# The Fourier part of a hybrid encoder layer: its last product turned round, with features in partitions and 257 frequencies

## The chip, the cores and the metric

The kernel runs on one core of a Trainium2 chip. The metric is the device time of one execution in microseconds (us); the time of a kernel is the median of its runs. PE is the TensorE matmul pipe and PEld its weight load, DVE is VectorE, ACT is ScalarE, POOL is GpSimd, and SP is SyncE, whose queue ("SPq") issues nearly all DMAs.

## The reference

One encoder layer on 512 tokens of 1024 features in float32: x gains W_out times the concatenation of three mixers of the normed x (gated linear attention, GLA, 256 features; Fourier, 256; latent attention, MLA, 512), and then a mixture of 32 experts is added. The Fourier mixer is this:

```python
def fnet_mixer(u, w_mix):            # u: 512 tokens x 256 features = 4 groups of 64
    uf = u.astype(jnp.float32).reshape(B, S, FNET_GROUPS, FNET_DG)
    f = jnp.fft.fft2(uf, axes=(1, 3), norm='ortho').real
    y = jnp.einsum('bsgc,gcd->bsgd', f, w_mix.astype(jnp.float32))
    return y.reshape(B, S, FNET_W).astype(u.dtype)

x = x + jnp.concatenate([o_gla, o_fnet, o_mla], axis=-1) @ w_out[l]
x = x + hier_moe(rms_norm(x, norm2_g[l]), ...)
```

The real part is C u Cc - S u Ss, where C and S are the cosine and sine transforms over the tokens and Cc and Ss those over the 64 channels of a group. Over the tokens C u is even and S u is odd about frequency 256.

## The kernel before, in words

Each engine runs a program of its own, written out in order (the `block.sync`, `block.tensor`, `block.scalar`, `block.vector` and `block.gpsimd` functions); semaphores join them. The eight PSUM banks are given out by a plan, `psum_plan` (line 69): `use(key, bank)` notes for every product its bank and how often the bank must have been filled and freed by then. `open_bank` waits until the product before in that bank was read, `filled` waits for a product, `free_bank` counts a read, and `drained(eng, key)` makes an engine wait until a product was read.

The order is: the input projection; GLA; the Fourier part and MLA; the output projection with W_out, tile by tile of 128 tokens, with the routing; the 32 experts in pairs, with the weights of 7 experts held at a time; the sum and the last norm.

The Fourier part. The tokens are folded in two halves (sum and difference), and four products `AB` (line 949) give cosine and sine transforms of two blocks of 128 features at 129 even or 128 odd frequencies. `spectrum` (line 565) is used by ScalarE (lines 1424 to 1428) and VectorE (`copy_spectrum`, line 1779) to copy each product twice into the tile `AB` (cosine or sine, block, 512 frequencies): once as it is and once mirrored for the upper frequencies. The matrices `fM` are the channel transforms multiplied by the mixing weights, with a third, negated copy of the sine one for the upper half. Behind the first set of scores TensorE forms `fy` (line 994): for each tile of 128 frequencies, with the frequencies in partitions, 2 blocks x 2 products of 128x128. ScalarE copies each tile to `MIX[:, t, 256:512]` (`copy_fy`, line 1430). GLA's output stands in `MIX[:, t, 0:256]`; GpSimd multiplies it by its gate there (line 2148) and raises `gla_out`.

MLA. `attention_order` (line 184) writes out TensorE's order: for each of 8 sets `s`, four score tiles of 128x512 (`scores`, line 974: a part without rope, one with, one without; lines 958 and 969), into banks 0 to 3. In sets 3 and 4 two transposes `mT` of MIX each follow (line 1030: 4 transposes per bank), which put the four blocks of 128 mixed features into partitions, for W_out. Then come the product with V for set s-2 (`AV`, line 1047) and the transposes of the probabilities of set s-1 (`PT`, line 1036). The `pre` steps, behind the last set, begin the output projection (line 1002). The other engines follow the same order by hand: VectorE takes each row's maximum (`row_max`, line 1804) and scales the probabilities (`normalise`, line 1808: a reciprocal at line 1810, a scaling at line 1811); ScalarE takes the exponentials (`exponent`, line 1434), which free banks 0 to 3, and copies the transposed probabilities (`copy_probs`, line 1442). The four `mT` products are copied to `xnT` by ScalarE (line 1461) and VectorE (line 1821).

SyncE waits at line 638 for the last `fy` tile to have been copied and for `gla_out`, and then issues the loads of the final gain, of W_out (lines 641, 642; over the tile AB), and of the weights of experts 2 and 3. It waits for the four `mT` (line 655) before it loads expert 4's gate and up weights over MIX, and then for the attention's outputs before the next loads.

Of the kernel before, what the change touches and what calls it, by code (L numbers as in the profile page):

```python
# [30 lines left out]
ALU = mybir.AluOpType  # L31
# [3 lines left out]
P = 128  # L35
# [21 lines left out]
PAIRS = NE // 2  # L57
SETS, MIX_TURNS = 8, (3, 4)

# [9 lines left out]
def psum_plan():  # L69
# [56 lines left out]
    for j in range(4):  # L126
        use(("S", j), j)
    for t in range(T):
        use(("fy", t), 4 + t)
    turn[0] = 0  # L130

    def middle(key):
        use(key, 4 + turn[0] % 3)
        turn[0] += 1

    for kind, i in attention_order():
        if kind == "S" and i:
            for j in range(4):
                use(("S", 4 * i + j), j)
        elif kind == "mT":  # L140
            middle(("mT", i))
        elif kind == "PT":
            middle(("PT", i))
        elif kind == "AV" and i % 2 == 0:
            use(("O", i // 2), 7, fill=0)
# [38 lines left out]
def attention_order():  # L184

    steps = []
    for s in range(SETS + 2):
        if s < SETS:  # L190
            steps.append(("S", s))
        if s in MIX_TURNS:
            steps += [("mT", 2 * MIX_TURNS.index(s) + c) for c in range(2)]
        if s >= SETS:
            steps.append(("pre", s - SETS))
        if s >= 2:
            steps.append(("AV", s - 2))
        if 1 <= s <= SETS:
            steps += [("PT", 4 * s - 4 + j) for j in range(4)]
    return steps + [("pre", 2)]  # L200
# [43 lines left out]
def encoder_kernel(nc, d, out):  # L244
    ctx = ExitStack()
    with ctx:
# [72 lines left out]
        qr2 = view(WO, 2064, (T, MH, 2, ROPE))  # L319
        AB = view(WO, 4112, (2, 2, S))  # L320
        gexp = view(WO, 6144, (2, 2, S))
# [11 lines left out]
        chan = view(ew01, 10496, (2, P))  # L333
        fM = view(ew01, 10752, (3, 2, P))
        rtmp = view(ew01, 11776, (4, MH, HALF))
# [24 lines left out]
        w_at.update({(k, 2): w_in_sb[:, 4 * k - 4:4 * k, GV:GV + 512] for k in (1, 2)})  # L360
        rrow = MIX[:, 0, 512:1024]
        rdiag = MIX[:, 1, 512:1024]
        ones = MIX[:, 2, 512:512 + P]
# [201 lines left out]
        def spectrum(i):  # L565

            odd, blk, n = i // 2, i % 2, ODD if i // 2 else EVEN
            ps = banks[PLAN[("AB", i)][0]][:, 0:2 * n].rearrange("p (a k) -> p a k", a=2)
            mirrored = ps[:, :, ODD - 1::-1] if odd else ps[:, :, ODD - 1:0:-1]
            return AB[:, :, blk, odd:S // 2 + 1:2], ps, AB[:, :, blk, S // 2 + 2 - odd:S:2], mirrored  # L570

# [19 lines left out]
        def _(sp):  # L591
# [45 lines left out]

            drained(sp, ("fy", T - 1))
            sp.wait_ge(gla_out, 1)
# [21 lines left out]
            load_down(3, 3)  # L661
            for c in range(4):
                drained(sp, ("mT", c))
# [92 lines left out]
        def _(pe):  # L756
# [232 lines left out]
            drained(pe, "M")  # L989
            for t in range(T):  # L990
                ps = open_bank(("fy", t))
                for blk in range(2):
                    for i in range(2):
                        mm = pe.matmul(ps[:, blk * P:(blk + 1) * P], AB[:, i, blk, t * P:(t + 1) * P],
                                       fM[:, 2 if i and t >= T // 2 else i, blk, :], start=(i == 0), stop=(i == 1))
                close_bank(mm, ("fy", t))
            for t in range(T):
# [11 lines left out]
            for kind, i in attention_order():  # L1009
# [3 lines left out]
                elif kind == "pre":  # L1013
                    if i == 0:
                        for c in range(4):
                            drained(pe, ("mT", c))
                        pe.wait_ge(wout_landed, 32)
                        out_part(0, 0, 0, 2)
                    elif i == 1:
                        out_part(0, 0, 2, 4)  # L1020
                    else:
                        out_part(0, 1, 0, 4)
                elif kind == "mT":
                    if i == 0:
                        pe.wait_ge(gla_out, 1)
                        for t in range(T):
                            drained(pe, ("fy", t))
                    ps = open_bank(("mT", i))
                    for t in range(T):
                        mm = pe.transpose(ps[:, t * P:(t + 1) * P], MIX[:, t, i * P:(i + 1) * P], ident[:, :])  # L1030
                    close_bank(mm, ("mT", i))
                elif kind == "PT":
# [273 lines left out]
        def _(act):  # L1306
# [103 lines left out]
            ps = filled(act, "M")  # L1410
            act.activation(fM[:, 0:2].rearrange("p a b n -> p (a b n)"), ps[:, :], ACT.Copy)
            free_bank(act.activation(fM[:, 2].rearrange("p b n -> p (b n)"), ps[:, 2 * P:], ACT.Copy, scale=-1.0), "M")
            def copy_rope(pair):
# [10 lines left out]
            for i in (0, 2):  # L1424
                filled(act, ("AB", i))
                low, ps, high, mirrored = spectrum(i)
                act.activation(high, mirrored, ACT.Copy)
                free_bank(act.activation(low, ps, ACT.Copy), ("AB", i))

            def copy_fy(t):  # L1430
                ps = filled(act, ("fy", t))
                free_bank(act.activation(MIX[:, t, 256:512], ps[:, 0:256], ACT.Copy), ("fy", t))

# [15 lines left out]

            for i in range(T):  # L1450
                exponent(i)
                copy_fy(i)
            for s in range(1, SETS + 1):
                ahead = 1 if s == 1 else 3
                for j in range(4):
                    if s < SETS:
                        exponent(4 * s + j)
                    if j == 1 and s in MIX_TURNS:
                        c = 2 * MIX_TURNS.index(s)
                        ps = filled(act, ("mT", c))  # L1460
                        free_bank(act.activation(xnT[:, c, :], ps[:, :], ACT.Copy), ("mT", c))
                    if j + 1 >= ahead:
                        copy_probs(4 * s - 4 + j + 1 - ahead)
                for j in range(5 - ahead, 4):
                    copy_probs(4 * s - 4 + j)
# [101 lines left out]
        def _(dve):  # L1567
# [211 lines left out]
            def copy_spectrum(i):  # L1779
                filled(dve, ("AB", i))  # L1780
                low, ps, high, mirrored = spectrum(i)
                dve.tensor_copy(high, mirrored)
                free_bank(dve.tensor_copy(low, ps), ("AB", i))

# [14 lines left out]
            def copy_heads(pair):  # L1799
                ps = banks[PLAN[("O", pair)][0]]  # L1800
                dve.wait_ge(av_done, 2 * pair + 2)
                free_bank(dve.tensor_copy(xnT[:, 4 + pair, :], ps[:, :]), ("O", pair))

            def row_max(i):
                ps = filled(dve, ("S", i))
# [7 lines left out]
            for s in range(SETS):  # L1813
                for j in range(4):
                    row_max(4 * s + j)
                    if j >= 2:
                        normalise(4 * s + j - 2)
                    if j == 2 and s in MIX_TURNS:
                        c = 2 * MIX_TURNS.index(s) + 1
                        ps = filled(dve, ("mT", c))  # L1820
                        free_bank(dve.tensor_copy(xnT[:, c, :], ps[:, :]), ("mT", c))
                for j in range(2, 4):
# [404 lines left out]
```

## Time and profile before

| | us |
|---|---|
| median of 3 runs | 511.85 (511.58 to 512.86) |
| the profiled execution | 512.89 |
| its span, first to last instruction | 511.1 |
| around the span | 1.79 |

| engine | busy us | share of the span |
|---|---|---|
| PE | 483.2 | 95% |
| DVE | 228.5 | 45% |
| ACT | 134.2 | 26% |
| POOL | 80.6 | 16% |

The busy share of an engine is an average over stages; what sets the pace of a stage is read from the chain of waits and the stretch itself. A TensorE product in float32 shows as two instructions, and a transpose as one. A bank is named "bank" whichever of the eight it is.

### The profile page before, as it was taken

The page shows a single profiled execution, that of the slowest core. Times are in us where ns is not written, and L with a number is a line of the kernel's source. Part 1 is how long each engine was busy: PE and PEld are TensorE (multiplying, and loading weights), DVE is VectorE, ACT ScalarE, POOL GpSimd, SP SyncE. Part 2 cuts the span into 40 slices and gives each one's busy share as a digit, 9 for nine tenths or more (in the row PEclk, how much of TensorE's full clock was granted, in tenths as well). Part 3 has the DMA queues.
Part 4 walks back from the last instruction along what each step waited for, and adds up shares of the span by engine and source line. Part 5 has one row for each costly group of instructions (what it writes and reads, how often), then busy time and mean ns, then how long its engine had stood idle before and what let it go on. Part 6 is the DMA issues. An engine that isn't in the chain of part 4 may idle for free.

```text
span 511.1 us, 7785 instructions
## 1 busy us (share of the span) xinstructions
PE 483.2 (95%) x2960; PEld 258.0 (50%) x2960; DVE 228.5 (45%) x573; ACT 134.2 (26%) x357; POOL 80.6 (16%) x100
## 2 busy tenths in 40 slices
PE   5999999999999999999989899999999997799894
PEld 4474444557554564445555455555555553354431
DVE  2498512866767631136663322222222222333167
ACT  3514202243666641122321011111111110112023
POOL 1013000083000000001320222222222222111000
PEclk9999999999999999999999999999999999989998
DMA  8996000000596008911599999999999999999974
GB/s 290 372 247 269 1 1 0 18 0 3 204 421 241 1 0 350 401 72 44 198 318 318 385 422 421 418 419 419 418 419 417 419 419 419 419 420 418 408 284 164
DMA packets 35206, 138.97 MB, mean 272 GB/s; under 512 B 9752, under 2 KB 11864, under 8 KB 23136
## 3 DMA queue, kind: packets, MB, share of 16 engines
q1 hardware_dynamic: 29824, 130.39, 65.0%
q0 software_dynamic: 4816, 7.85, 4.1%
q8 instruction: 24, 0.39, 0.3%
q10 hardware_dynamic: 528, 0.22, 0.2%
q14 instruction: 14, 0.11, 0.1%
HBM read 129.94 MB, written 16.39 MB: 286 GB/s over the span
## 4 chain that ended last, share of the span: by engine, by line
PE 80%; DMA 11%; DVE 4%; SPq 3%; issue 1%; ACT 1%; DVEq 0%; POOLq 0%; ACTq 0%
PE bank L1140 19%; PE bank L1002 10%; PE bank L819 9%; PE bank L1153 9%; DMA EW<-in_moe_w_up 6%; PE bank L958 3%; PE bank L1036 3%; PE bank L1047 3%; PE bank L1112 3%; DMA EW<-y_scratch 2%; PE bank L969 2%; DMA EW<-in_w_in 2%; PE bank L780 2%; SPq L648 2%; PE bank L788 1%; PE bank L897 1%
## 5 line engine op out<-in xcount | busy, mean ns | idle before, releaser
L1140 PE MATMUL bank<-EW,WO 128*64 128x256 f32 x640 | 76.9, 391 | 5.9 <-DMA EW<-in_moe_w_up 3.3
L1140 PEld LDWEIGHTS bank<-EW,WO 128*64 128x64 f32 x640 | 44.1, 134 | 33.3 <-DMA EW<-in_moe_w_up 5.4
L1002 PE MATMUL bank<-WO,XT 128*128 128x512 f32 x128 | 56.9, 596 | 0.0
L1935 DVE TENSOR_TENSOR G<-G,bank 128x128 f32<-128x128 f32 x32 | 9.2, 288 | 104.6 <-ACT G L1514 104.6
L1514 ACT ACTIVATE G<-bank 128x128 f32<-128x128 f32 x32 | 8.9, 278 | 177.9 <-PE bank L1140 177.9
L2161 POOL DMA_INDIRECT y_scratch<-G,sidx x30 | 30.3, 1010 | 153.4 <-DVE G L1948 138.0
L1948 DVE COPY G<-bank 128x512 f32<-128x512 f32 x32 | 22.1, 692 | 46.4 <-PE bank L1153 44.6
L1153 PE MATMUL bank<-EW,G 128*64 128x512 f32 x160 | 38.3, 599 | 0.0
L1002 PEld LDWEIGHTS bank<-WO,XT 128*128 128x128 f32 x128 | 23.6, 190 | 26.9 <-issue 26.9
L2155 POOL DMA_INDIRECT list_scratch<-lrow,dest x8 | 7.9, 990 | 130.9 <-DVE dest L1892 129.7
L1439 ACT ACTIVATE G<-bank,nm 128x512 f32<-128x512 f32 x32 | 21.9, 687 | 14.4 <-PE bank L969 7.8
L1806 DVE TENSOR_REDUCE nm<-bank 128x1 f32<-128x512 f32 x32 | 20.7, 685 | 8.2 <-PE bank L969 7.9
L1504 ACT ACTIVATE WO<-bank,gain 128x128 f32<-128x128 f32 x64 | 18.3, 369 | 14.2 <-PE bank L1112 14.2
L1447 ACT ACTIVATE EW<-bank 128x512 f32<-128x512 f32 x32 | 17.5, 606 | 8.2 <-PE bank L1036 8.1
L1140 PE MATMUL bank<-XT,WO 128*64 128x256 f32 x128 | 17.0, 421 | 2.2 <-DMA XT<-in_moe_w_up 2.2
L1650 DVE SCALAR_TENSOR_TENSOR EW<-bank,stat,EW 128x512 f32<-128x512 f32 x10 | 7.5, 751 | 24.8 <-PE bank L819 24.3
L1851 DVE TENSOR_TENSOR X<-bank,X 128x512 f32<-128x512 f32 x8 | 5.5, 691 | 28.5 <-PE bank L1002 28.5
L1153 PEld LDWEIGHTS bank<-EW,G 128*64 128x64 f32 x160 | 10.4, 135 | 15.6 <-issue 13.2
L958 PE MATMUL bank<-EW 64*128 64x512 f32 x64 | 18.1, 641 | 0.0
L1140 PE MATMUL bank<-MIX,WO 128*64 128x256 f32 x128 | 15.4, 391 | 1.9 <-DMA MIX<-in_moe_w_up 1.9
L1140 PE MATMUL bank<-WO 128*64 128x256 f32 x128 | 15.4, 391 | 1.7 <-DMA WO<-in_moe_w_up 1.7
L1146 PEld LDWEIGHTS bank<-ident,G 128*128 128x128 f32 x32 | 4.4, 139 | 24.7 <-issue 22.7
(317 smaller groups left out, 743.3 us busy)
## 6 DMA issues: line engine op xcount, KB each, us to landing
EW<-in_moe_w_down SPq DMA_DIRECT2D x20, 1024.0 KB, 25.9
EW<-in_moe_w_gate SPq DMA_DIRECT2D x19, 1024.0 KB, 19.8
EW<-in_moe_w_up SPq DMA_DIRECT2D x19, 1024.0 KB, 24.0
y_scratch<-MIX SPq DMA_DIRECT2D x8, 512.0 KB, 8.4
WO<-in_w_out SPq DMA_DIRECT2D x2, 2048.0 KB, 11.7
MIX<-in_moe_w_gate SPq DMA_DIRECT2D x4, 1024.0 KB, 16.8
MIX<-in_moe_w_up SPq DMA_DIRECT2D x4, 1024.0 KB, 20.7
G<-in_moe_w_down SPq DMA_DIRECT2D x4, 1024.0 KB, 25.3
```

What stands on the lines that cost most here:

```text
L819: mm = pe.matmul(ps[:, :], a[:, c, unit * P:(unit + 1) * P], w[:, c, :], start=(c == 0 and product in (1, 6, 5)), stop=(c == 3), skip_grou ...
L958: mm = pe.matmul(ps[:, :], qn[rows, pair, tq * P:(tq + 1) * P], kn[rows, pair, :], start=(tile == 0), stop=(tile == 1))
L1002: mm = pe.matmul(ps[:, :], xnT[:, c, t * P:(t + 1) * P], w_out_sb[:, c, n * 512:(n + 1) * 512], start=(c == 0), stop=(c == C - 1))
L1036: mm = pe.transpose(ps[:, kc * P:(kc + 1) * P], probs[:, i % 8, kc * P:(kc + 1) * P], ident[:, :])
L1140: mm = pe.matmul(bank[BLOCK * m:BLOCK * (m + 1), 0:2 * P].rearrange("p (w n) -> p w n", w=2), xeT[:, c, par * BLOCK:(par + 1) * BLOCK], wv ...
L1153: mm = pe.matmul(bank[BLOCK * q:BLOCK * (q + 1), :], hT[:, par, m, :], wv[:, m, q * 512:(q + 1) * 512], start=(m == 0), stop=(m == 1))
L1439: free_bank(act.activation(probs[:, i % 8], ps[:, :], ACT.Exp, bias=nm[:, i:i + 1], accum_out=rs[:, i:i + 1]), ("S", i))
L1447: free_bank(act.activation(probsT[:, g, u, :, tile * P:(tile + 1) * P], ps[:, :].rearrange("p (k n) -> p k n", k=T), ACT.Copy), ("PT", j))
L1504: ins = act.activation(xeT[:, c], banks[half][:, j * P:(j + 1) * P], ACT.Copy, scale=gain2[:, c:c + 1])
L1806: dve.tensor_reduce(nm[:, i:i + 1], ps[:, :], AX, ALU.max, negate=True).then_inc(neg_max, 1)
L1948: dve.tensor_copy(Y[:, e % 2], banks[4 + e % 2][:, :]).then_inc(y_ready, 1)
L2161: pool.indirect_dma_start(y_rows, bass.IndirectOffsetOnAxis(ap=sidx[:, col:col + 1], axis=0), Y[:, e % 2], None, bounds_check=4 * S - 1, o ...
```

## The change

TensorE's last Fourier product is turned round: fM is the stationary operand and AB the moving one, so the result has features in partitions and frequencies along the row, as W_out needs it. Only the 257 frequencies from 0 to 256 are formed: one bank `sines` (2 blocks of 256, without frequency 0, where the sine is zero) and two banks `cosines` (257 each). ScalarE copies the sines to a spare part of MIX. VectorE's `mirror`, in set 1 behind the second and the fourth row maximum, writes the feature block to xnT: frequency 0, cosines plus sines for 1 to 256, and mirrored cosines minus mirrored sines for 257 to 511. So `AB` keeps its lower half, the mirrored copies go (ScalarE's and VectorE's, two each), and the negated third part of fM goes.

The `mT` transposes are left for GLA's two blocks alone. They move to right behind the cosines, with TensorE's wait for `gla_out` in front, and both are copied by ScalarE ahead of set 1. The plan gives sines bank 4, cosines banks 7 and 5, the transposes 6 and 4, and the transposed probabilities turn through 6, 4, 5. SyncE's wait for the last `fy` becomes one for the two cosine banks, which `mirror` frees, and its wait for four `mT` becomes one for two. The waits for `mT` and the cosines stand ahead of the first `pre` step too.

```diff
@@ def psum_plan(): which bank each product goes to @@
-    for t in range(T):
-        use(("fy", t), 4 + t)
+    use("sines", 4)
+    for blk in range(2):
+        use(("cosines", blk), (7, 5)[blk])
+    for c in range(2):
+        use(("mT", c), (6, 4)[c])
     turn[0] = 0

     def middle(key):
-        use(key, 4 + turn[0] % 3)
+        use(key, (6, 4, 5)[turn[0] % 3])
         turn[0] += 1
...
-        elif kind == "mT":
-            middle(("mT", i))
@@ def attention_order() @@
         if s < SETS:
             steps.append(("S", s))
-        if s in MIX_TURNS:
-            steps += [("mT", 2 * MIX_TURNS.index(s) + c) for c in range(2)]
@@ tiles @@
-        AB = view(WO, 4112, (2, 2, S))
+        AB = view(WO, 4112, (2, 2, S // 2 + 1))
-        fM = view(ew01, 10752, (3, 2, P))
+        fM = view(ew01, 10752, (2, 2, P))
+        sines = MIX[:, 0, 512:1024].rearrange("p (b k) -> p b k", b=2)
@@ def spectrum(i) @@
-            mirrored = ps[:, :, ODD - 1::-1] if odd else ps[:, :, ODD - 1:0:-1]
-            return AB[:, :, blk, odd:S // 2 + 1:2], ps, AB[:, :, blk, S // 2 + 2 - odd:S:2], mirrored
+            return AB[:, :, blk, odd:S // 2 + 1:2], ps
@@ SyncE @@
-            drained(sp, ("fy", T - 1))
+            for blk in range(2):
+                drained(sp, ("cosines", blk))
             sp.wait_ge(gla_out, 1)
...
-            for c in range(4):
+            for c in range(2):
                 drained(sp, ("mT", c))
             sp.wait_ge(y_zeroed, 16 * 2 * T)
             load_gate_up(RING, RING)
@@ TensorE, behind scores(0) @@
-            for t in range(T):
-                ps = open_bank(("fy", t))
-                for blk in range(2):
-                    for i in range(2):
-                        mm = pe.matmul(ps[:, blk * P:(blk + 1) * P], AB[:, i, blk, t * P:(t + 1) * P],
-                                       fM[:, 2 if i and t >= T // 2 else i, blk, :], start=(i == 0), stop=(i == 1))
-                close_bank(mm, ("fy", t))
+            ps = open_bank("sines")
+            for blk in range(2):
+                mm = pe.matmul(ps[:, blk * 256:(blk + 1) * 256], fM[:, 1, blk, :], AB[:, 1, blk, 1:], start=True, stop=True)
+            close_bank(mm, "sines")
+            for blk in range(2):
+                ps = open_bank(("cosines", blk))
+                close_bank(pe.matmul(ps[:, 0:S // 2 + 1], fM[:, 0, blk, :], AB[:, 0, blk, :], start=True, stop=True),
+                           ("cosines", blk))
+            pe.wait_ge(gla_out, 1)
+            for c in range(2):
+                ps = open_bank(("mT", c))
+                for t in range(T):
+                    mm = pe.transpose(ps[:, t * P:(t + 1) * P], MIX[:, t, c * P:(c + 1) * P], ident[:, :])
+                close_bank(mm, ("mT", c))
...
-                elif kind == "mT":
-                    if i == 0:
-                        pe.wait_ge(gla_out, 1)
-                        for t in range(T):
-                            drained(pe, ("fy", t))
-                    ps = open_bank(("mT", i))
-                    for t in range(T):
-                        mm = pe.transpose(ps[:, t * P:(t + 1) * P], MIX[:, t, i * P:(i + 1) * P], ident[:, :])
-                    close_bank(mm, ("mT", i))
@@ ScalarE @@
-            act.activation(fM[:, 0:2].rearrange("p a b n -> p (a b n)"), ps[:, :], ACT.Copy)
-            free_bank(act.activation(fM[:, 2].rearrange("p b n -> p (b n)"), ps[:, 2 * P:], ACT.Copy, scale=-1.0), "M")
+            free_bank(act.activation(fM.rearrange("p a b n -> p (a b n)"), ps[:, :], ACT.Copy), "M")
...
             for i in (0, 2):
                 filled(act, ("AB", i))
-                low, ps, high, mirrored = spectrum(i)
-                act.activation(high, mirrored, ACT.Copy)
-                free_bank(act.activation(low, ps, ACT.Copy), ("AB", i))
-
-            def copy_fy(t):
-                ps = filled(act, ("fy", t))
-                free_bank(act.activation(MIX[:, t, 256:512], ps[:, 0:256], ACT.Copy), ("fy", t))
+                out, ps = spectrum(i)
+                free_bank(act.activation(out, ps, ACT.Copy), ("AB", i))
...
-            for i in range(T):
+            for i in range(4):
                 exponent(i)
-                copy_fy(i)
+                if i == 0:
+                    ps = filled(act, "sines")
+                    free_bank(act.activation(sines.rearrange("p b k -> p (b k)"), ps[:, :], ACT.Copy), "sines")
+            for c in range(2):
+                ps = filled(act, ("mT", c))
+                free_bank(act.activation(xnT[:, c, :], ps[:, :], ACT.Copy), ("mT", c))
...
-                    if j == 1 and s in MIX_TURNS:
-                        c = 2 * MIX_TURNS.index(s)
-                        ps = filled(act, ("mT", c))
-                        free_bank(act.activation(xnT[:, c, :], ps[:, :], ACT.Copy), ("mT", c))
@@ VectorE @@
+            def mirror(blk):
+                ps = filled(dve, ("cosines", blk))
+                drained(dve, "sines")
+                out = xnT[:, 2 + blk, :]
+                dve.tensor_copy(out[:, 0:1], ps[:, 0:1])
+                dve.tensor_tensor(out[:, 1:257], ps[:, 1:257], sines[:, blk, :], ALU.add)
+                free_bank(dve.tensor_tensor(out[:, 257:], ps[:, 255:0:-1], sines[:, blk, 254::-1], ALU.subtract),
+                          ("cosines", blk))
...
                     row_max(4 * s + j)
                     if j >= 2:
                         normalise(4 * s + j - 2)
-                    if j == 2 and s in MIX_TURNS:
-                        c = 2 * MIX_TURNS.index(s) + 1
-                        ps = filled(dve, ("mT", c))
-                        free_bank(dve.tensor_copy(xnT[:, c, :], ps[:, :]), ("mT", c))
+                    if s == 1 and j % 2:
+                        mirror(1 if j == 1 else 0)
```

## Rows read from the trace of the kernel before

**Rows 1.** The page: engine shares, and GB/s in the 40 slices of 12.8 us.
```profile
...
PE 483.2 (95%) x2960; PEld 258.0 (50%) x2960; DVE 228.5 (45%) x573; ACT 134.2 (26%) x357; POOL 80.6 (16%) x100
...
GB/s 290 372 247 269 1 1 0 18 0 3 204 421 241 1 0 350 401 72 44 198 318 318 385 422 421 418 419 419 418 419 417 419 419 419 419 420 418 408 284 164
```

**Rows 2.** Chain of waits, 120 to 192 us: start, length, engine, tile, line, instructions.
```profile
...
121.02 3.47 PE bank L949 x16
...
127.68 3.77 PE bank L994 x32
131.45 1.06 PE bank L958 x4
...
134.64 1.99 PE bank L1036 x16
...
137.71 1.16 PE bank L969 x6
...
138.90 1.12 PE bank L969 x2
...
148.14 1.02 PE bank L1030 x8
...
182.30 1.72 PE bank L1002 x4
```

**Rows 3.** Timeline of ScalarE, 126 to 140 us: start, length, line, idle before.
```profile
...
128.81 0.39 ACT L1432 ACTIVATE MIX<-bank 128x256 f32<-128x256 f32 x1 [0.60 <-PE bank L994]
...
134.39 0.69 ACT L1439 ACTIVATE G<-bank,nm 128x512 f32<-128x512 f32 x1 [2.36 <-DVE nm L1806]
...
135.26 0.60 ACT L1447 ACTIVATE EW<-bank 128x512 f32<-128x512 f32 x1
...
138.04 0.72 ACT L1439 ACTIVATE G<-bank,nm 128x512 f32<-128x512 f32 x1
```

**Rows 4.** Lines of VectorE by shape, 80 to 200 us: busy us, mean ns.
```profile
...
L1806 DVE TENSOR_REDUCE nm<-bank 128x1 f32<-128x512 f32 x32 | 20.7, 685 | 8.2 <-PE bank L969 7.9 <-PE bank L958 0.3
...
L1810 DVE RECIPROCAL ri<-rs 128x1 f32<-128x1 f32 x32 | 5.1, 158 | 6.1 <-ACT G L1439 6.1
...
L1790 DVE TENSOR_TENSOR MIX<-bank,rgla 128x256 f32<-128x256 f32 x4 | 1.4, 417 | 0.0
...
L1782 DVE COPY WO<-bank 128x256 f32<-128x256 f32 x1 | 0.4, 417 | 0.0
...
L1811 DVE TENSOR_SCALAR G<-G,ri 128x512 f32<-128x512 f32 x32 | 15.6, 486 | 1.1
```

**Rows 5.** Timeline of GpSimd, 120 to 130 us.
```profile
...
125.21 2.35 POOL L2148 TENSOR_TENSOR MIX<-MIX,EW 128x1024 f32<-128x1024 f32 x1 [7.84 <-DVE MIX L1790]
```

**Rows 6.** Lines of GpSimd by shape, whole run: busy us, mean ns.
```profile
...
L2114 POOL TENSOR_TENSOR EW<-EW,ropet 128x128 f32<-128x128 f32 x4 | 2.3, 580 | 12.2 <-ACT EW L1398 12.0
```

**Rows 7.** Timeline of SyncE's queue, 118 to 200 us: the DMA issues.
```profile
...
132.05 0.35 SPq L640 DMA_DIRECT2D G<-in_final_norm_g  x1
...
158.41 0.33 SPq L648 DMA_DIRECT2D MIX<-in_moe_w_gate  x1
...
192.32 0.33 SPq L648 DMA_DIRECT2D EW<-in_moe_w_gate  x1
```

**Rows 8.** The page, DMA issues: KB each, median us from issue to landing.
```profile
...
WO<-in_w_out SPq DMA_DIRECT2D x2, 2048.0 KB, 11.7
```

**Rows 9.** Stretches: busy time by engine, granted clock, DMA share, GB/s.
```profile
...
134.64:136.63 1.99, 1.99 (x19) 1.71 (x18) 1.96 (x6) 1.89 (x6) 0.00 (x0) 1.00 0.76 274
...
446.00:448.20 2.20, 0.04 (x2) 0.00 (x1) 1.74 (x6) 0.00 (x0) 0.90 (x1) 1.00 0.99 400
448.20:452.00 3.80, 3.80 (x20) 2.21 (x22) 0.00 (x0) 0.00 (x0) 0.17 (x1) 0.55 1.02 419
```

**Rows 10.** Timeline of TensorE, 438 to 458 us.
```profile
...
440.22 3.84 PE L1140 MATMUL bank<-WO 128*64 128x256 f32 x32 [1.65 <-DMA WO<-in_moe_w_up]
...
448.20 5.44 PE L1140 MATMUL bank<-XT,WO 128*64 128x256 f32 x32 [2.16 <-DMA XT<-in_moe_w_up]
```

More of the change, by code:

```diff
@@ L57 @@
 PAIRS = NE // 2
-SETS, MIX_TURNS = 8, (3, 4)
+SETS = 8
 OVB = S // BLOCK
@@ L1014, in _ @@
                     if i == 0:
-                        for c in range(4):
+                        for c in range(2):
                             drained(pe, ("mT", c))
+                            drained(pe, ("cosines", c))
                         pe.wait_ge(wout_landed, 32)
@@ L1448, in copy_probs @@
                                          ps[:, :].rearrange("p (k n) -> p k n", k=T), ACT.Copy), ("PT", j))
-            for i in range(T):
+            for i in range(4):
                 exponent(i)
-                copy_fy(i)
+                if i == 0:
+                    ps = filled(act, "sines")
+                    free_bank(act.activation(sines.rearrange("p b k -> p (b k)"), ps[:, :], ACT.Copy), "sines")
+            for c in range(2):
+                ps = filled(act, ("mT", c))
+                free_bank(act.activation(xnT[:, c, :], ps[:, :], ACT.Copy), ("mT", c))
             for s in range(1, SETS + 1):
@@ L1780, in copy_spectrum @@
                 filled(dve, ("AB", i))
-                low, ps, high, mirrored = spectrum(i)
-                dve.tensor_copy(high, mirrored)
-                free_bank(dve.tensor_copy(low, ps), ("AB", i))
+                out, ps = spectrum(i)
+                free_bank(dve.tensor_copy(out, ps), ("AB", i))
             copy_rope(3)
```

## The prediction

> **What bounds the kernel now.** Read the engine shares first: TensorE is busy for 95% of the span, no other engine for half of it [rows 1]. Such a share can hide waits, so the chain of waits is read next, in order of time, around the change. From 121.02 to 192 us it lies on TensorE, each piece beginning where the one before ends; the reader is to see the five pieces that the change touches or meets [rows 2]: the transforms AB, the 32 instructions of line 994 (3.77 us), the score sets (131.45 to 134.64, so 3.19 us a set), the transposes of probabilities, and the transposes of MIX (1.02 us in set 3; a second such piece stands in set 4). There is one wait, in set 2: six of the eight rope instructions stand at 137.71, and the last two begin only at 138.90 and last to 140.02. A part of a set takes about 1.06 us (its first does); this one took 2.31, so about 1.2 us are lost. ScalarE's timeline gives the reason: the exponential that frees bank 3 starts at 138.04, and TensorE goes on 0.86 us later [rows 2, 3]. So in this stretch TensorE sets the pace, and once, in set 2, ScalarE does.
>
> Then the DMA slices: about 0 GB/s from 166 to 192 us, and 417 to 422 from 294 to 473 us [rows 1]. The first load after the idle stretch is issued at 192.32, when the attention's last outputs have been copied [rows 7]. The expert stage therefore starts when the attention ends, and its stream of weights with it.
>
> **TensorE, what goes.** 32 instructions of line 994: 3.77 us. Two pieces of MIX transposes in sets 3 and 4: 2 x 1.02 = 2.04 us [rows 2]. Together 5.81.
>
> **TensorE, what comes.** Sines and cosines are 4 products, 8 instructions of 256 or 257 columns on a 128x128 stationary tile. Line 949 ran that shape: 16 instructions in 3.47 us, 0.217 each, so 8 are 1.73 us [rows 2]. (From the other side: 128 columns took 3.77 / 32 = 0.118 there, twice that is 0.236, and 8 are 1.89.) I take 1.73. The transposes of GLA's two blocks are 8, one piece of the old kind: 1.02. Together 2.75. **The sum: 5.81 - 2.75 = 3.06 us less**, of which 3.77 - 2.75 = 1.02 is gained in front of set 1, and 1.02 in each of sets 3 and 4.
>
> **Can TensorE be that early?** Sines begin at 127.68, cosines end at 129.41, transposes run to 130.43, set 1 begins there and not at 131.45.
> - GLA's output. The wait for `gla_out` now stands at 129.41, and behind it on TensorE's queue stand the transposes and all of set 1, for which everything later waits. GpSimd's multiply runs from 125.21 for 2.35 us, to 127.56 [rows 5]: 1.85 us to spare. Its spans are rough: at the rate of the dearest multiply (580 ns for 128 elements, so 4.64 us for 1024 [rows 6]) it ends at 129.85, a wait of 0.45. The latest possible is 132.05, when SyncE, which waits for it too, issued its load [rows 7]: 2.64. So 0 to 2.64; I take 0.
> - Bank 4, for the second transposes, wanted at 129.92. The sines' bank is full at 128.55. ScalarE took the first `fy` 0.19 us after its quarter of line 994 was done (128.62, 128.81), so it starts at 128.74; a copy of 512 columns is 0.60 [rows 3], to 129.34. No wait.
> - Banks 1 to 3 for set 1. The exponentials follow that copy at 129.34, 130.03 and 130.72 (0.69 each), and free a bank 0.86 after their start [rows 3]: 130.2, 130.9, 131.6. The banks are wanted at 130.43 (1) and 1.06 later, 131.49 (2, 3). 0 to 0.1; I take 0.
> - The two ScalarE copies of the transposes follow the third exponential: 131.4 to 132.6. The next exponential waits for VectorE until 134.39 - 1.02 = 133.37, as it waited 2.36 us before [rows 3]. Hidden; 0.8 us to spare.
>
> **VectorE in set 1.** A `mirror` is a copy of one column (0.16, by the reciprocal of one column), an add and a subtraction of 256 columns from PSUM (0.417 each, line 1790; reading backwards cost no more in line 1782 [rows 4]): 1.0 us. From above it is three instructions of the dearest kind in that set, 0.685 each: 2.1. In set 1 the first row maximum ends as its exponential starts, at 133.37 - 0.09, the second at 133.97, the first mirror at 134.97. TensorE wants bank 5, which it frees, for the third transposed tile at 133.62 + 1.0 = 134.62: it waits up to 0.35. That is paid out of the 1.2 us which it loses in set 2 anyway, as long as ScalarE is not late. Behind the mirror stand the third maximum (to 135.66), a normalise (0.16 + 0.49, to 136.31) and the fourth maximum (to 137.0). Their exponentials were at 136.90 and 138.04 and are wanted 1.02 earlier, at 135.88 and 137.02 [rows 3]. So the slack is 0.2 and 0.0 with every duration laid end to end, and rather more as instructions overlap a little. I take no loss; at 2.1 us a mirror it would be 1.1. Then come a normalise and the second mirror, to 138.65; bank 7, which it frees, is wanted by the first AV product behind set 2, at 140.02 + 1.06 - 1.02 = 140.06. Two more normalises and the first maximum of set 2 end at 140.6, and its exponential has freed bank 0 at 141.6. Set 3 wants it at 148.14 - 3.19 - 1.02 = 143.93 [rows 2].
>
> **Copies that go.** Two mirrored copies on ScalarE (0.39 each by line 1432 [rows 3]) and two on VectorE (0.417 [rows 4]), the negated fM, three of four `fy` copies, and the `mT` copies of sets 3 and 4. All lay beside TensorE's pieces: 0 us. If that cover were gone they could only save.
>
> **SyncE's queue.** The wait for the cosines ends with the second mirror, so gain, W_out and the four loads behind them (7 DMAs, 8.5 MB) are issued from about 138.7 and not 132.05. At the 421 GB/s of that slice [rows 1] they are done by about 159; W_out, whose issue to landing took 11.7 us [rows 8], by about 151. It is wanted at 182.30 - 3.06 = 179.2. Expert 4's two loads follow at once instead of at 158.41 [rows 7]. All is landed by about 165, as now, and the queue then waits for the attention. 0 us, with 28 us of cover for W_out.
>
> **The end.** Everything behind the attention is started by it, so the 3.06 us are handed through. The profiled execution took 512.89 (span 511.1, around it 1.79), which makes 509.83 (span 508.0). It is 1.04 above the median of 511.85, so for a median: **508.8 us**.
>
> **A rule against the change.** The stretch of 16 transposes ran at a granted clock of 1.00 (2.4 GHz) and so did what followed it [rows 2, 9]. The Trainium skill ("TensorE: Matmul & The Clock Gate", Part 4) says that transposes do not count as busy time for the clock; the change puts 8 transposes where matmuls were. By that rule set 1 would run at half clock and its 3.19 us would double: 512.0, no gain. The trace speaks against it, so it gets 0.02.
>
> **The rivals.**
> - A, ScalarE's wait in set 2 eats the first 1.02. For: slack of 0.0 to 0.2, and VectorE has 2 us more in set 1. Against: the first exponential of set 1 waited 2.36 us for its maximum, and that for its scores (VectorE's idle time ahead of line 1806 ends with line 969 [rows 3, 4]), so this whole chain moves with TensorE. 511.85 - 2.04 = 509.8. Chance 0.15.
> - B, `gla_out` is late: 508.8 plus 0.45 to 2.64, 509.2 to 511.4. Against: 1.85 us to spare. 0.05.
> - C, slower. TensorE waits at `gla_out` and its clock falls. When it had waited 2.16 us for weights (446.0 to 448.2) the granted clock fell to 0.5 (1.2 GHz; 0.55 over 448.2 to 452), and 32 instructions of line 1140 took 5.44 us, where they took 3.84 at 440.22: 1.6 lost [rows 9, 10]. With a wait of 2.64: 508.8 + 2.64 + 1.6 = 513.0, with two such falls 514.6. It decides from a wait of 1.5 us, `gla_out` at 130.9 or later. 0.05.
> - D, the weights' stream sets the end and does not move: 511.8. For: 418 GB/s without a gap for 180 us. Against: it is idle from 166 to 192 and started by the attention. 0.06.
>
> **How the numbers follow.** Forecast 0.67, A 0.15, B 0.05, C 0.05, D 0.06, the rule 0.02. A measurement here can tell 0.3%, 1.5 us, from no change: faster means below 510.3. Forecast and A less 0.02 for the spread of medians: 0.80. B, D, the rule and that spread: 0.15. C: 0.05. The range goes down to 507.6, where the 1.2 us lost in set 2 would vanish too, and up to 511.4, the end of B; it leaves out C, D and the rule.
>
> **What would show it.** Line 1030's transposes in one piece of 1.0 us near 129.4 and none in sets 3 and 4; sines and cosines in 1.73; set 1 at 130.4; the same 1.2 us wait in set 2; the first load after the attention at 189.3; a span near 508.0. Wrong: TensorE idle ahead of the transposes, a wait of over 2 us in set 2, or sets 1 to 4 earlier and the first expert not.

## The result, and the profile after

The changed kernel takes 509.8 us (median of 11 runs, 508.09 to 511.37), the kernel before beside it 512.36 us (median of 11, 511.15 to 513.53). The ratio is 0.9944, 95% interval 0.9931 to 0.9957: on 512.36 us that is 2.87 us less (2.2 to 3.5); the two medians themselves lie 2.56 apart. 508.8 was predicted, 3.06 less than the median of the three runs that were known then (511.85). The profiled execution took 509.01, its span is 507.2. Two runs of this record, one of E4 (815 us) and one of the kernel before beside E3 and E4 (558 us), ran as a whole at a far lower granted clock (0.56 and 0.85) and are left out of the times and ratios.

The page first: TensorE's busy time fell from 483.2 to 479.4 [rows 1].

```profile
PE 479.4 (95%) x2928; PEld 254.2 (50%) x2928; DVE 227.6 (45%) x575; ACT 132.3 (26%) x351; POOL 80.4 (16%) x100
```

The chain of waits, 119 to 192 us (start, length, engine, tile, line, instructions):

```profile
127.87 1.06 PE bank L992 x4
128.93 0.87 PE bank L996 x4
129.80 0.87 PE bank L1002 x8
130.67 1.06 PE bank L958 x4
...
133.86 1.02 PE bank L1035 x8
...
134.98 1.06 PE bank L1035 x8
...
137.10 2.13 PE bank L969 x8
...
188.65 3.63 PE bank L1009 x8
```

The reader is to see, against [rows 2], that 127.87 (sines), 128.93 (cosines) and 129.80 (the eight transposes, now line 1002) follow each other without a gap: 1.06 + 0.87 + 0.87 = 2.80 us where 3.77 stood. Set 1 runs from 130.67 to 133.86, 3.19 us. One gap of 0.10 us stands ahead of the third transposed tile (134.98). The middle part of set 2 took 2.13 us, where the one of set 1 takes 1.07; in the kernel before it took 2.31 [rows 2], so the wait in it is still there. The first product of the output projection behind the attention starts at 188.65 (it started at 191.49). From the first sine to that product it is 60.78 us; from the first product of line 994 to it, it was 63.81. **The stretch lost 3.03 us; the sum said 3.06.** (TensorE came into the stretch 0.19 later than before, 127.87 against 127.68; in the traces of the experiments, which all contain the change, it comes in between 127.50 and 128.06.)

VectorE's timeline in set 1 (start, length, line, operation, idle before):

```profile
132.82 1.29 DVE L1808 TENSOR_REDUCE nm<-bank 128x1 f32<-128x512 f32 x2 [0.53 <-PE bank L969]
134.03 0.15 DVE L1801 COPY XT<-bank 128x1 f32<-128x1 f32 x1
134.09 0.41 DVE L1802 TENSOR_TENSOR XT<-bank,MIX 128x256 f32<-128x256 f32 x1
134.42 0.41 DVE L1803 TENSOR_TENSOR XT<-bank,MIX 128x255 f32<-128x255 f32 x1
134.75 0.68 DVE L1808 TENSOR_REDUCE nm<-bank 128x1 f32<-128x512 f32 x1
```

The first mirror is the copy, the addition and the subtraction at 134.03, 134.09 and 134.42. The next maximum starts at 134.75: 0.72 us from start to start, not the 1.0 of their durations, since each instruction starts before the one ahead of it has ended (0.33 from one to the next of 0.41).

SyncE's issues:

```profile
137.97 0.35 SPq L640 DMA_DIRECT2D G<-in_final_norm_g  x1
...
143.54 1.13 SPq L648 DMA_DIRECT2D MIX<-in_moe_w_gate  x1
...
189.48 0.33 SPq L648 DMA_DIRECT2D EW<-in_moe_w_gate  x1
...
296.38 0.33 SPq L648 DMA_DIRECT2D MIX<-in_moe_w_gate  x1
```

The wait for the cosines ends at 137.97 (138.7 was expected), expert 4's weights follow at 143.54 and not 158.41, and the first load behind the attention is issued at 189.48: 2.84 us earlier than 192.32 [rows 7]. The shift is still 2.86 at the next load into `MIX` (296.38), which the kernel before issued here (SyncE's timeline):

```profile
299.24 0.33 SPq L648 DMA_DIRECT2D MIX<-in_moe_w_gate  x1
```

What follows depends on that stream. TensorE's products that wait for their weights, after:

```profile
427.72 3.85 PE L1139 MATMUL bank<-MIX,WO 128*64 128x256 f32 x32 [2.01 <-DMA MIX<-in_moe_w_up]
```

and before:

```profile
431.51 3.84 PE L1140 MATMUL bank<-MIX,WO 128*64 128x256 f32 x32 [1.89 <-DMA MIX<-in_moe_w_up]
```

This one starts 3.79 us earlier, a later one of the kind 3.90 (478.15 against 482.05). The load issued at 296.38 (299.24) and the product that waits for it (427.72, 431.51) are 131.34 us apart after and 132.27 before: 0.93 us that no instruction of the change touches. Over the experiments below, which all contain the change, the same distance is 130.70 (E1), 130.71 (E2), 130.72 (E3), 130.53 (E4), 130.96 (E5), 131.55 (E6) and 131.56 (E7), without order by what was altered. The runs of one kernel spread by over 2 us. Between the traces, this stream's pace differs by up to 1.7 us; that it also makes the spread of one kernel's runs is likely, but each kernel has one trace only, so it is not shown.

### The profile page after: what moved, and what is told of

Same layout as the page of the kernel before. It is cut to its first block, busy times and chain, and to the rows that moved or that the text cites. A ratio compares the mean times of both kernels' runs of the same rounds, so it can differ in the third digit from the quotient of the medians.

```text
span 507.2 us, 7716 instructions
## 1 busy us (share of the span) xinstructions
PE 479.4 (95%) x2928; PEld 254.2 (50%) x2928; DVE 227.6 (45%) x575; ACT 132.3 (26%) x351; POOL 80.4 (16%) x100
## 4 chain that ended last, share of the span: by engine, by line
PE 81%; DMA 11%; DVE 4%; SPq 2%; issue 1%; ACT 1%; DVEq 0%; POOLq 0%; ACTq 0%
PE bank L1139 19%; PE bank L1009 10%; PE bank L819 9%; PE bank L1152 9%; DMA EW<-in_moe_w_up 6%; PE bank L958 3%; PE bank L1035 3%; PE bank L1046 3%; PE bank L1111 3%; DMA EW<-y_scratch 2%; DMA EW<-in_w_in 2%; PE bank L969 2%; PE bank L780 2%; PE bank L788 1%; PE bank L897 1%; DMA y_scratch<-G,sidx 1%
## 6 DMA issues: line engine op xcount, KB each, us to landing
WO<-in_w_out SPq DMA_DIRECT2D x2, 2048.0 KB, 12.8
```

## The experiments

Two theories stood against each other: **the sum** (every piece of TensorE's work counts its own time, wherever it stands) and **the banks** (the new place of the transposes is worth more, because without them TensorE would wait for score banks). The others put a number on the mirrors, the gate and the copies. "The stretch" is the one above, from the first sine to the output projection: 60.78 us.

**E1: GLA's transposes back in set 3,** with the wait for `gla_out`; sines and cosines stay.

```diff
 # TensorE, behind the cosines
-            pe.wait_ge(gla_out, 1)
-            for c in range(2):
-                ps = open_bank(("mT", c))
...
 # order of the parts
+        if s == 3:
+            steps += [("mT", c) for c in range(2)]
```

> The changed kernel, but GLA's eight transposes (and the wait for GLA's output) go back behind the scores of set 3. Measure: the time from the first sines product to the first product of the output projection behind the attention, 60.78 us in the changed kernel (127.87 to 188.65), 63.81 in the kernel before. Sum theory (the prediction's: TensorE is the pace everywhere here, a moved piece costs the same elsewhere): 60.8 to 60.9. Theory of the banks: set 1 would begin at 129.80, but bank 1 is free only 0.86 us after the second exponential starts (129.46), at 130.3, and bank 3 at 131.6, so the transposes stood in a wait and were nearly free there; set 1 gains 0.1 us and set 3 pays 1.0: 61.5 to 61.8.

Measured: 509.63 us, one run. Its chain, same columns:

```profile
127.86 1.06 PE bank L994 x4
...
129.79 1.61 PE bank L960 x4
131.40 1.34 PE bank L971 x8
...
133.80 1.99 PE bank L1038 x16
...
147.29 1.02 PE bank L1032 x8
...
189.72 2.34 PE bank L1005 x5
```

The stretch is 189.72 - 127.86 = 61.86, 1.08 more than with the transposes in front. The reader is to see 129.79 and 131.40: the first two parts of set 1 take 1.61 and 1.34, where they took 1.06 and 1.07, and the transposes now cost 1.02 at 147.29. So set 1 took 0.82 us longer, as it would if it waited for banks that the exponentials had not freed; E5 puts that to the test. Of the 1.08 us, 0.82 is this, 0.15 the dearer transposes, and 0.10 the first piece of the output projection inside the attention (1.82 us and not 1.72), for which the traces show no reason. The banks were right (61.5 to 61.8 was expected) and the sum wrong (60.8 to 60.9): in the changed kernel the transposes stand in time that TensorE would otherwise lose.

**E5: E1, and the sines copied one exponential later,** so that the exponentials free banks earlier.

```diff
-                if i == 0:
+                if i == 1:
                     ps = filled(act, "sines")
```

> The kernel of e1 (GLA's transposes behind set 3), and ScalarE copies the sines behind its second exponential instead of its first, so that banks 1 to 3 are free about 0.7 us earlier. e1's stretch from the sines to the output projection was 61.86 us, and its set 1 took 4.0 us instead of 3.2. Theory of the banks: set 1 takes 3.2 to 3.4 and the stretch 61.1 to 61.3. If e1's set 1 was slow for another reason (the change from full products to half-array ones, say), the sines' place changes nothing: 61.9.

Measured: 509.44 us, one run. The chain:

```profile
128.06 1.06 PE bank L994 x4
...
129.99 1.06 PE bank L960 x4
131.05 1.22 PE bank L971 x8
...
133.33 2.04 PE bank L1038 x16
...
189.25 2.77 PE bank L1005 x6
```

Set 1 takes 3.34 us (129.99 to 133.33) and not the 4.01 of E1, and the stretch 61.19, both as the banks said. Nothing but ScalarE's order was altered against E1, so it is the 0.60 us copy of the sines ahead of the exponentials that held the banks. With that copy out of the way the late transposes cost 0.41 us, not 1.08.

**E2: each mirror's addition and subtraction done twice,** the first time into a spare place.

```diff
+                dve.tensor_tensor(MIX[:, 1, at:at + 256], ps[:, 1:257], sines[:, blk, :], ALU.add)
+                dve.tensor_tensor(MIX[:, 2, at:at + 255], ps[:, 255:0:-1], sines[:, blk, 254::-1], ALU.subtract)
                 dve.tensor_tensor(out[:, 1:257], ps[:, 1:257], sines[:, blk, :], ALU.add)
```

> The changed kernel with the add and the subtraction of each mirror done twice, the extra results into an unused part of MIX. Each mirror is 0.66 us longer (0.33 from start to start each). Prediction's arithmetic with durations laid end to end (no slack behind the mirror): the wait in set 2 grows by all of it, 60.78 becomes 61.4. With the overlaps that the changed kernel's trace shows (third exponential's maximum has 0.6 us in hand, the fourth's 0.5): 0.1 to 0.2 us longer, 60.9 to 61.0; TensorE waits about 0.66 longer ahead of the third transposed tile of set 1, and that is taken off its wait in set 2.

Measured: 508.8 us, one run; the stretch 61.12 (127.64 to 188.76), 0.34 more. TensorE's timeline:

```profile
135.41 1.06 PE L1035 MATMUL bank<-ident,G 128*128 128x128 f32 x8 [0.75 <-DVE XT L1806]
...
137.46 1.64 PE L969 MATMUL bank<-EW 32*128 32x512 f32 x8
...
141.97 2.31 PE L1035 MATMUL bank<-ident,G 128*128 128x128 f32 x16
```

The last row is the transposed tiles of set 2. In the changed kernel the middle part of set 2 is this in the same view:

```profile
137.03 2.20 PE L969 MATMUL bank<-EW 32*128 32x512 f32 x8
```

And the chain of E2 at the end of set 2:

```profile
143.02 0.50 ACT EW L1440
...
143.65 0.63 PE bank L1035 x4
```

Each mirror grew by 0.66 us (four instructions 0.33 apart). TensorE waited 0.75 for bank 5 ahead of the third transposed tile, 0.65 more than in the changed kernel, but its middle part of set 2 took 1.64 and not 2.20, so 0.56 came back. As predicted for bank 5, a wait there is paid out of the one in set 2. The rest of the 0.34 stands in the transposed tiles of set 2, which take 2.31 us and not 2.06 (142.10 in the changed kernel): their last four transposes come behind a copy by ScalarE, as the chain shows. ScalarE is late there because the first exponential of set 2 is. In E2:

```profile
140.90 0.69 ACT L1432 ACTIVATE G<-bank,nm 128x512 f32<-128x512 f32 x1 [2.48 <-issue]
```

and in the changed kernel:

```profile
139.82 0.69 ACT L1432 ACTIVATE G<-bank,nm 128x512 f32<-128x512 f32 x1 [1.27 <-issue]
```

Counted from the first sine it starts 13.26 us behind and not 11.95, 1.31 later, which is both mirrors' 0.66. The 0.34 is thus more than the 0.1 to 0.2 expected, because of the second mirror, and not the whole 0.66 of the other theory. What sets the wait in set 2 of the changed kernel is ScalarE's own order: from 133.60 to the fourth exponential at 137.25 its exponentials and copies follow each other without idle time. VectorE had time in hand there: with 0.66 us more in the first mirror, the third and fourth exponentials of set 1 start only 0.07 and 0.13 later, counted from the first sine (135.96 and 137.15 in E2, 136.12 and 137.25 in the changed kernel).

**E7 and E3: `gla_out` later,** by two and by four more multiplies of 512 elements on GpSimd.

```diff
+            for _ in range(2):      # E7; E3 has 4
+                link(pool.tensor_tensor(spare, MIX[:, 0:2, 0:256], vg[:, 0:2, 256:512], ALU.mult))
             pool.tensor_tensor(MIX[:, :, 0:256], MIX[:, :, 0:256], vg[:, :, 256:512], ALU.mult).then_inc(gla_out, 1)
```

> The changed kernel with two extra GpSimd multiplies of 512 elements ahead of GLA's gating (e3 had four): the output comes 2.7 us later, near 130.4, and TensorE waits 0.7 us at the transposes. In e3 TensorE stood for 3.5 us and its granted clock then fell to about 0.5, 1.6 us more. Theory: a wait of 0.7 is handed through and the clock stays: stretch 61.5. If any wait here brings the clock down: 63.1. If the wait in set 2 covers it: 60.8.

> The changed kernel with four extra GpSimd multiplies of 512 elements (1.2 us each) ahead of GLA's gating, so that its output is signalled about 4.8 us later, near 132.5, and TensorE, which wants it at 129.8, waits 2.7 us. Rival B of the prediction: the wait is handed through, the stretch from the sines to the output projection is 63.5 and the end 2.7 us later. Rival C: the granted clock also falls to 0.5 behind the wait, set 1 and what follows is slower by about 1.6 us: 65.1. If the wait were covered by the later wait in set 2 (1.07 us): 62.4.

Measured, E7: 510.19 us, one run; the stretch 61.79 (127.82 to 189.61), 1.0 more (61.5 was expected). E3: 515.46 us (median of 10 runs, 512.25 to 517.31), ratio to before 1.0053 (1.0027 to 1.0079), so slower than before. TensorE's timeline (idle before and what ended it in brackets), E7:

```profile
130.44 1.09 PE L1002 MATMUL bank<-ident,MIX 128*128 128x128 f32 x8 [0.69 <-POOL MIX L2151]
```

and E3:

```profile
133.18 1.09 PE L1002 MATMUL bank<-ident,MIX 128*128 128x128 f32 x8 [3.48 <-POOL MIX L2151]
```

and the chain of E3 behind it:

```profile
134.28 2.01 PE bank L958 x4
136.28 1.73 PE bank L969 x8
```

The granted clock by stretch (start and end, length; busy time and instructions of PE, PEld, DVE, ACT and POOL; granted clock; DMA share; GB/s), E7:

```profile
130.50:132.00 1.50, 1.50 (x11) 1.09 (x12) 1.43 (x6) 0.99 (x4) 0.00 (x0) 1.00 0.00 0
```

and E3:

```profile
133.20:134.20 1.00, 1.00 (x8) 0.84 (x8) 0.77 (x3) 0.32 (x1) 0.00 (x0) 0.99 0.00 0
134.20:138.00 3.80, 3.80 (x15) 1.07 (x14) 0.00 (x0) 0.76 (x2) 0.00 (x0) 0.55 0.00 0
```

A wait of 0.69 us for GpSimd cost its length and 0.3 us more, at a clock that stayed at 1.00: 0.22 because the transposes took 1.09 behind the wait and not 0.87, and 0.10 in the first piece of the output projection, as in E1. After a wait of 3.48 us the transposes still ran at 0.99, and then the clock was 0.55 from 134.20 to 138.00, about the lower of its two levels (1.2 GHz). The first two parts of set 1 took 2.01 and 1.73 us and not 1.06 and 1.07, 1.61 us lost. The output projection came at 193.96 (the row of E3's chain below); from the first sine at 127.77 the stretch took 66.19 us, 5.41 more: the wait of 3.48, the slow parts' 1.61, and the same 0.3 as in E7. (In E7 and E3 the chain passes through GpSimd and not the sines; their start is the timeline's, 127.75 and 127.70, and 0.07, by which a piece starts later in the chain: 127.80 and 127.87 in the changed kernel.)

```profile
193.96 2.34 PE bank L1009 x5
```

The multiplies took 1.28 us each with 0.07 between them, so the wait is 3.48 and not the expected 2.7; the price of the fall is the 1.6 of rival C.

**E6: the mirrored copies put back,** 250 columns with each of the four spectra.

```diff
-            return AB[:, :, blk, odd:S // 2 + 1:2], ps
+            mirrored = ps[:, :, 124::-1]
+            return AB[:, :, blk, odd:S // 2 + 1:2], ps, WO[:, at:at + 250].rearrange("p (a k) -> p a k", a=2), mirrored
 # ScalarE, and in the same way VectorE with dve.tensor_copy
+                act.activation(high, mirrored, ACT.Copy)
                 free_bank(act.activation(out, ps, ACT.Copy), ("AB", i))
```

> The changed kernel with a second, mirrored copy of 250 columns put back for each of the four products AB (two on ScalarE, two on VectorE, into an unused part of W_out's tile). The prediction priced the copies that went at nothing because TensorE was busy with set 0 beside them: the stretch stays 60.8, to 0.1. If they had a part in the gain: up to 0.8 us more, 61.6.

Measured: 509.07 us, one run. The chain's end of the stretch:

```profile
127.77 1.06 PE bank L994 x4
...
188.56 3.63 PE bank L1011 x8
```

60.79 us, as without them (60.78), and the sines do not start later either (127.77; 127.87 in the changed kernel): beside TensorE's work these copies cost nothing. For the other copies that went (of fM, fy and mT) there is no run.

**E4: a filler for the wait in set 2.** One block of cosines and one block of transposes moved between the second and third transposed tile of set 1, and the sines copied behind the second exponential, as in E5. The bank plan is fitted to it.

```diff
-            for blk in range(2):
-                ps = open_bank(("cosines", blk))
...
+            cosine_block(1)
             pe.wait_ge(gla_out, 1)
-            for c in range(2):
-                ps = open_bank(("mT", c))
...
+            gla_block(0)
 # order of the parts, set 1
+            steps[-2:-2] = [("mT", 1), ("cosines", 0)]
```

> The changed kernel, with the second cosine block and the second four transposes moved in between the second and the third transposed tile of set 1, where TensorE has 1.07 us in hand before ScalarE frees bank 3; ScalarE copies the sines behind the second exponential instead of the first, so that banks 1 to 3 are free 0.7 us earlier. Theory of the banks: set 1 begins 0.7 to 0.87 us earlier and the wait in set 2 shrinks by as much: 60.0 to 60.2 where the changed kernel has 60.78, and 0.6 to 0.8 us off the end, too little for the clock of a run to show (0.1%). Sum theory: TensorE's instructions are the same, 60.8.

Measured: 508.70 us (median of 11 runs), ratio to before 0.9933 (0.9908 to 0.9959); the stretch 60.16 (127.50 to 187.66). TensorE's timeline:

```profile
135.29 0.63 PE L1047 MATMUL bank<-ident,G 128*128 128x128 f32 x4 [0.19 <-ACT EW L1452]
...
136.91 1.24 PE L973 MATMUL bank<-EW 32*128 32x512 f32 x8
```

The middle part of set 2 takes 1.24 (136.91) and not 2.20 (E2's rows, 137.03 of the changed kernel), and 0.19 is waited ahead of the last transposed tiles. The stretch is 0.62 us shorter than in the changed kernel, as the banks said (60.0 to 60.2), not as the sum said (60.8). It is the shortest of all kernels here. The filler and the later copy were altered together, so what each gave is not taken apart. Whether its end is earlier than the changed kernel's is not settled: 0.9933 and 0.9944 lie well within each other's interval, and 0.62 us is less than what the weights' stream differs by from trace to trace.

## Why the prediction was right, step by step

- **The sum on TensorE.** 3.06 predicted, 3.03 measured, and by the path that was named: the pieces of line 994, and two pieces of transposes, gone from a stretch that TensorE paces. Of its terms, sines and cosines took 1.93 and not 1.73: the cosines 0.87, as line 949's rate gave, but the sines, four instructions of the same shape, 1.06. The transposes took 0.87 and not 1.02. The two errors, 0.20 and 0.15, nearly cancel, and that the sum came out at 0.03 is in part luck. In E1, where the transposes follow score products, they took 1.02 again, and a first piece behind score products is 0.15 to 0.19 us dearer in both places. The prediction took one price for a piece; it depends on what stood ahead of it: the transposes took 1.02 behind scores, 0.87 behind cosines, and 1.09 behind a wait (E7, E3).
- **`gla_out`.** Cost 0, as taken: GpSimd's multiply ended at 127.73 and was wanted at 129.80, so 2.07 us to spare. E7 and E3 show what it costs without that cover.
- **Banks 1 to 4.** Set 1 without a wait, as worked out. What the prediction did not draw from its own times: the exponentials free bank 1 at 130.2, and TensorE is through with the cosines at 129.4. Without the transposes in between set 1 takes 0.82 us longer (E1). So the sum holds only at this place; the same instructions in set 3 make a stretch 1.08 us longer.
- **The mirrors and the wait in set 2.** 1.0 us a mirror was taken, 0.72 measured, because of the overlaps; bank 5 was waited for 0.10 and not up to 0.35. The transposed tiles of set 1 took 2.18 with that wait and not 1.99, and set 2 lost 1.07 where it had lost 1.2: the 0.19 came back, and the wait went along with TensorE, as argued against rival A. The slack "0.0 to 0.2" was mis-sized, because durations were laid end to end: E2 put 0.66 into each mirror, 0.07 and 0.13 of it reached the two exponentials for which the slack was worked out, and 0.34 the end of the stretch.
- **Copies that go, SyncE's loads.** 0 for both; E6 shows it for the mirrored copies, and the loads behind the cosines cost nothing, as TensorE does not wait for `WO` at its first product from it (179.47), nor at 188.65.
- **The absolute time.** 508.8 was worked out from a median of three runs, 511.85. Eleven runs beside the result give 512.36, so the same 3.06 less would be 509.3; 509.8 was measured.
- **Handing through.** The first load behind the attention was 2.84 earlier; the time by runs 2.87 (2.2 to 3.5). The profiled pair alone says 3.88 (512.89 to 509.01), of which 0.93 is the weights' stream. Why that stream takes 130.5 to 132.3 us from one run to the next is open; no run took it apart. The stream in the single profile of before is the longest of nine, so a small part that belongs to the change can't be excluded, but the interval of the runs leaves at most 0.5 for it (3.5 less 3.03).
- **The rivals.** A: set 2's wait did not grow. B: no wait for `gla_out`. C: true as a mechanism, E3 shows its price, but in the changed kernel TensorE does not wait for `gla_out` at all. D: the stream moved with the attention. The rule against the change: set 1 behind the eight transposes ran in 3.19 us and did not double. The Trainium skill ("TensorE: Matmul & The Clock Gate", Part 4) says that transposes do not count as busy time as other products do; the granted clock over set 1 was 1.00:

```profile
130.67:133.86 3.19, 3.19 (x18) 0.92 (x18) 2.59 (x7) 2.13 (x7) 0.00 (x0) 1.00 0.00 0
```

So what the prediction worked out from that rule did not come. The rule itself is not settled by it: in E7 0.69 us without any work, and eight transposes behind it, left the clock at 1.00 as well.

## What to carry to other kernels

Where one engine sets the pace, a sum of its instructions' times is a good forecast, but only where the instructions stand in an order in which it does not wait; work out for each place when its buffers come free, and put pieces that need nothing into the holes (by place alone 1.08 us between E1 and the changed kernel, and 0.41 where the banks come earlier, in E5). A wait that another engine's order sets, as in set 2, moves along with the whole and can be filled (0.62 us in E4, with the earlier banks). A late input is paid about once while the clock stays (0.69 us of wait cost 1.0), and a second time, in slow products behind it, when the clock falls (3.48 us of wait cost 5.4).

## What the runs showed of the hardware that was not expected

VectorE's scaling from SBUF to SBUF waits for a running GpSimd multiply. It takes 0.49 us; in E7 and E3 it took 1.90 and 2.38 (VectorE, then GpSimd; start, length), E7:

```profile
128.77 1.90 DVE L1813 TENSOR_SCALAR G<-G,ri 128x512 f32<-128x512 f32 x1
```

```profile
128.03 2.35 POOL L2151 TENSOR_TENSOR MIX<-MIX,EW 128x1024 f32<-128x1024 f32 x1
```

and E3:

```profile
131.04 2.38 DVE L1813 TENSOR_SCALAR G<-G,ri 128x512 f32<-128x512 f32 x1
```

```profile
130.73 2.40 POOL L2151 TENSOR_TENSOR MIX<-MIX,EW 128x1024 f32<-128x1024 f32 x1
```

In both it ends 0.29 us behind GpSimd's instruction (130.38 and 130.67; 133.13 and 133.42), while row maxima, which read PSUM, ran beside GpSimd at their usual 0.68. The Trainium skill ("SBUF — State Buffer", section "SBUF: two separate sides") describes such a lock on the port pair that the two engines share, held for a whole instruction; the trace agrees. In the changed kernel the multiply ends at 127.73, ahead of the first scaling, and the lock costs nothing. In E7 it put off the fourth exponential (131.36), but set 1 still took 3.19 us.

The clock: 0.69 us of idle TensorE left it at 1.00, 3.48 us took it to 0.55, and not at once: eight transposes behind the wait were still at 0.99. Between these, the length of the wait alone did not decide. The same product behind the same wait for weights, in E1 and in E2:

```profile
444.89 5.45 PE L1142 MATMUL bank<-XT,WO 128*64 128x256 f32 x32 [2.18 <-DMA XT<-in_moe_w_up]
```

```profile
443.94 3.84 PE L1139 MATMUL bank<-XT,WO 128*64 128x256 f32 x32 [2.18 <-DMA XT<-in_moe_w_up]
```

Over the 3.80 us behind the wait the granted clock was 0.63 in E1 and 1.00 in E2. Of the nine traces, seven have the slow form of this product (waits of 1.85 to 2.19 us) and two the fast one (E2, and E4 with 2.20). The 1.6 us are not lost at the end there: the stream of weights took 130.70 us in E1 and 130.71 in E2. What decides, beside the wait, the runs do not show, so a price like rival C's holds for a fall that comes and does not say when it comes.
